# Activation tiles begin 64 bytes later in SBUF, weight tiles stay where they are

## The chip, the cores and the metric

One core of one Trainium2 chip runs the kernel. The metric is the device time of one execution in microseconds. Lower is better.

## The reference

Two transformer-like blocks on 512 tokens of width 1024, all in float32. In short:

```python
h = ln(ALPHA*x + 0.5*swiglu(x))                 # ffn1, 1024 -> 2816 -> 1024
h = ln(ALPHA*h + token_mixers(h))               # hgrn2 scan (4 heads) and spatial gating, then w_out
h = ln(ALPHA*h + cross_attention(h, ln(mem)))   # memory of 256 rows, 4 heads of 256
h = ln(ALPHA*h + 0.5*swiglu(h))                 # ffn2
z = modulate(h, c) @ w_in                       # second block: 11 slices of 512 and three gates of 1024
kc, vc = na_kv(modulate(ctx, c_ctx) @ w_in_kv)  # context of 256 rows
ya = neighbourhood_attention(q, k, v, kc, vc, rpb) * silu(..)
yb, yc = short_conv_branch(z), conformer_branch(z)
x = h + gate * ((ga*(ya@oa) + gb*(yb@ob) + gc*(yc@oc)) @ w_o)
```

Nearly all of the arithmetic is in the projections (`x @ w`).

## The kernel before

Activations are kept with features on the 128 partitions: a chunk is 128 features x 512 tokens, and `h` has 8 such chunks. The weights are streamed from HBM in strips of 128 x 1024 floats (512 KB), through a ring of four slots (`RING = 4`). There are some 300 strips. SyncE issues the load of a strip into `raw` when the strip four places before it has been split. ScalarE copies the strip to `w_hi` in the type fp32r (L407), and VectorE writes the remainder `raw - w_hi` to `w_lo` (L414). The activations are split in the same way into a `_hi` and a `_lo` tile.

A product of two float32 operands is then three fp32r matmuls, hi x hi, hi x lo and lo x hi, which accumulate in one bank of PSUM. All of them are issued by the helper `product`, in line L422. `feature_strip` runs the 8 blocks of a strip, so 24 matmuls: the 128 x 128 weight block is loaded into the array (the profile calls it PEld) and 512 or 256 columns of activations stream past it. In `token_strip` the roles are swapped, the activation block is loaded and the weights stream (`moving_weights`). In the names of the profile the moving operand stands first: `proj<-a_hi,w_hi` streams `a_hi` past `w_hi`.

The order of the work is written out by hand for each engine. TensorE goes through the strips in the order of the stream: gate and up of the first feed-forward (from 6 us), down, the mixer's projections with the scan's small matmuls between them, `w_out`, memory keys (`side_hi`, `side_lo`, 256 columns), memory values, queries, attention, `xa_w_o`, the context's keys (`ctx_hi`, `ctx_lo`, 256 columns, from 762 us), the second feed-forward, the context's values, twelve strips for each of four head pairs with the neighbourhood attention between them (up to 1462 us), the merge and `w_o`. The norms between the phases run on VectorE, ScalarE and GpSimd beside the last strips of the phase before; in some places a chunk is split into two halves of 256 tokens, which gives the 256-column matmuls of `a`, `hid` and `m`.

Tiles lie in SBUF in the order in which they are allocated. Tiles of an `ExitStack` named `ph` or `part` are released at its end, so the phases lie on top of each other, all behind `ctxv`. A tile takes its size in bytes for each partition, rounded up to 32. `raw`, `w_hi`, `w_lo` and `h` come first, 16,384 bytes each, and begin at an address that is a multiple of 128. `a_hi`, `a_lo` and then `cols` (271 floats, 1,084 bytes) follow. `consts` (1,024 bytes, its first half the identity) and the constant matrices behind it therefore begin at remainder 64 by 128. The small tiles behind them sum up so that `work`, `sq`, `ctxk`, `ctxv` and the tiles of all phases begin at remainder 0 again, with few exceptions: `ctx_hi` and `ctx_lo` at 64, behind `xs` with its 192 bytes, and in the attention phase the tiles from `glu` to `ns` at 32, behind `cv` with its 514 floats.

Of the kernel before, what the change touches and what calls it, by code (L numbers as in the profile page):

```python
# [20 lines left out]
F32 = mybir.dt.float32  # L21
# [6 lines left out]
P = 128  # L28
# [28 lines left out]
LEVELS = 7  # L57
RING = 4
SB = 8


S_FFN1 = 0
# [95 lines left out]
def hybrid_blocks(nc, stream, ada_in, cond_in, x_in, mem_in, ctx_in, cols_in, const_in, mask_in, rows_in, wst_in, band_in, rpb_in,  # L158
                  out):
    with ExitStack() as ctx:  # L160
# [3 lines left out]
        def sb(name, shape, dt=F32, scope=ctx):  # L164
            return scope.enter_context(nc.sbuf_tensor(name, shape, dt))
# [5 lines left out]

        raw = sb("raw", [P, RING, SB * P])
        w_hi = sb("w_hi", [P, RING, SB * P], F32R)
        w_lo = sb("w_lo", [P, RING, SB * P], F32R)
        h = sb("h", [P, KD, T])
        with ExitStack() as ph:
            cond_row = sb("cond_row", [P, 2, D], F32, ph)
            ada_prod = sb("ada_prod", [P, 2, D], F32, ph)
# [51 lines left out]
        with ExitStack() as ph:  # L230
            side = sb("side", [P, KD, M], F32, ph)
            side_hi = sb("side_hi", [P, KD, M], F32R, ph)
            side_lo = sb("side_lo", [P, KD, M], F32R, ph)
            xq = sb("xq", [P, KD, T], F32, ph)
            memk = sb("memk", [P, KD, M], F32, ph)
            memv_hi, memv_lo = (sb(n, [P, MB, W5], F32R, ph) for n in ("memv_hi", "memv_lo"))
            xp = sb("xp", [P, 2, 2, M], F32, ph)
            xpt_hi, xpt_lo = (sb(n, [P, 2, MB, M], F32R, ph) for n in ("xpt_hi", "xpt_lo"))
            xs = sb("xs", [P, 3, 8, 2], F32, ph)
            ctx_hi = sb("ctx_hi", [P, KD, M], F32R, ph)  # L240
            ctx_lo = sb("ctx_lo", [P, KD, M], F32R, ph)
        with ExitStack() as ph:
# [181 lines left out]

        def feature_strip(pe, st, g, xh, xl, first=0, blocks=SB, last=True, order=None, ready=None, n=T, blk0=0,
                          beside=None):

            pe.wait_ge(lo_ready, st.n + 1)
            if first == 0:
                ge(pe, proj_read[g.slot], g.turn)  # L430
            for j, k in enumerate(order or range(blocks)):
                if ready:
                    ready(k)
                if beside and k in beside:
                    beside[k]()
                at = (blk0 + k) * P
                mm = product(proj[:, g.slot, :n], w_hi[:, st.slot, at:at + P], w_lo[:, st.slot, at:at + P],
                             xh[:, first + k], xl[:, first + k], first == 0 and j == 0, last and j == blocks - 1)
            mm.then_inc(strip_done, 1)
# [483 lines left out]
        def pe_down(pe, s0, g0, hid0, m, beside):  # L923
            for c in range(KD):
                if c in beside:
                    beside[c]()
                for j in range(DOWN_STRIPS):
                    if c == 0:
                        pe.wait_ge(hid_l, hid0 + min(KF, SB * (j + 1)))
                    feature_strip(pe, Nth(s0 + c * DOWN_STRIPS + j), Nth(g0 + c), hid_hi, hid_lo, first=SB * j,  # L930
                                  blocks=min(SB, KF - SB * j), last=(j == DOWN_STRIPS - 1))
# [1814 lines left out]
```

## Time and profile before

| | |
|---|---|
| median of 3 runs | 1708.28 us (1707.93 to 1708.65) |
| profiled execution: span of its instructions | 1706.6 us |
| TensorE busy (matmuls) | 1691.5 us, 99% |
| weight loads, beside the matmuls | 1394.7 us, 82% |
| VectorE busy | 994.7 us, 58% |
| ScalarE busy | 683.6 us, 40% |
| GpSimd busy | 166.8 us, 10% |
| read from HBM | 182.9 MB, 110 GB/s |

The profile gives no other time for its own execution than the span. A matmul's end is modelled: successive matmuls of one strip overlap in the listing, each with a duration longer than its distance to the next one. So a full TensorE row says that matmuls followed each other without a pause, not that they went as fast as they can. For that one looks at the number of matmuls in a stretch, at the distance of their starts, or at differences of the durations.

### The profile page before, as it was taken

What the parts mean: (1) busy time and instruction counts of PE and PEld (TensorE: products, weight loads), DVE (VectorE), ACT (ScalarE), POOL (GpSimd) and SP (SyncE); (2) the same over time, 40 slices, a digit from 0 to 9 for tenths busy, and PEclk for the clock granted to TensorE, in tenths of its full rate; (3) what the DMA queues carried; (4) which work ended last, traced back from release to release, by engine and by line L of the source; (5) the groups of instructions that cost most, each with busy time, mean ns of one, the idle gap of its engine ahead of it and who ended that gap; (6) DMA issues with size and microseconds to landing.
All of it is one profiled execution on the core that took longest, in us unless ns stands there. A gap on an engine that the chain in (4) does not pass through costs nothing.

```text
span 1706.6 us, 22901 instructions
## 1 busy us (share of the span) xinstructions
PE 1691.5 (99%) x8500; PEld 1394.7 (82%) x8500; DVE 994.7 (58%) x1341; ACT 683.6 (40%) x975; POOL 166.8 (10%) x158
## 2 busy tenths in 40 slices
PE   9999999999999999999999999999999999999999
PEld 7888888888787888888888888877778787788887
DVE  5333339987965784666333333457976869844442
ACT  4222232246454465434222223346454445732330
POOL 0000000112004521013000000013011020000000
DMA  5333247633122353223332233323333222243331
GB/s 216 98 98 98 91 138 231 222 121 119 52 98 66 109 182 137 67 82 123 98 98 94 92 130 117 109 87 118 85 99 95 86 83 86 74 123 109 104 109 62
DMA packets 51476, 188.05 MB, mean 110 GB/s; under 512 B 5776, under 2 KB 6288, under 8 KB 50512
## 3 DMA queue, kind: packets, MB, share of 16 engines
q1 hardware_dynamic: 44640, 161.50, 29.7%
q10 hardware_dynamic: 5184, 16.00, 2.9%
q0 software_dynamic: 1584, 9.60, 1.6%
q8 instruction: 47, 0.77, 0.2%
q14 instruction: 21, 0.17, 0.0%
HBM read 182.89 MB, written 4.19 MB: 110 GB/s over the span
## 4 chain that ended last, share of the span: by engine, by line
PE 89%; DVE 7%; ACT 2%; issue 1%; DMA 0%; POOL 0%; SPq 0%; DVEq 0%; ACTq 0%; POOLq 0%
PE proj L422 83%; DVE w_lo L414 1%; PE aux L1859 1%; PE aux L1846 1%; PE aux L1619 1%; PE aux L1836 1%; DVE y L2016 0%; ACT w_hi L407 0%; DVE score L1221 0%; DVE qk L1264 0%; DVE md L1242 0%; PE aux L566 0%; DVE qk L1265 0%; PE aux L1839 0%; DVE md L1241 0%
## 5 line engine op out<-in xcount | busy, mean ns | idle before, releaser
L414 DVE TENSOR_TENSOR w_lo<-raw,w_hi 128x1024 fp32r<-128x1024 f32 x300 | 380.5, 1270 | 388.8 <-ACT w_hi L407 382.0
L422 PE MATMUL proj<-a_hi,w_hi 128*128 128x512 f32 (+1 forms) x1536 | 600.8, 391 | 3.3 <-DVE a_lo L909 1.8
L422 PE MATMUL proj<-a_hi,w_lo 128*128 128x512 f32 (+1 forms) x1536 | 591.3, 385 | 0.0
L422 PE MATMUL proj<-a_lo,w_hi 128*128 128x512 f32 (+1 forms) x1536 | 591.0, 385 | 0.0
L407 ACT ACTIVATE w_hi<-raw 128x1024 fp32r<-128x1024 f32 x300 | 315.3, 1053 | 233.4 <-PE proj L422 164.3
L422 PEld LDWEIGHTS proj<-a_hi,w_hi 128*128 128x128 f32 x1536 | 288.5, 188 | 67.9 <-issue 5.8
L422 PEld LDWEIGHTS proj<-a_lo,w_hi 128*128 128x128 f32 x1536 | 288.7, 188 | 58.4 <-issue 2.9
L422 PEld LDWEIGHTS proj<-a_hi,w_lo 128*128 128x128 f32 x1536 | 288.5, 188 | 58.5
L422 PE MATMUL proj<-hid_hi,w_hi 128*128 128x512 f32 (+1 forms) x374 | 142.6, 381 | 0.0
L422 PE MATMUL proj<-hid_hi,w_lo 128*128 128x512 f32 (+1 forms) x374 | 140.9, 377 | 0.0
L422 PE MATMUL proj<-hid_lo,w_hi 128*128 128x512 f32 (+1 forms) x374 | 140.8, 377 | 0.0
L971 ACT ACTIVATE hid_hi<-work 128x512 f32 (+1 forms) x44 | 27.8, 632 | 196.5 <-DVE work L988 196.5
L988 DVE TENSOR_TENSOR work<-sq,proj 128x512 f32<-128x512 f32 x44 | 30.2, 687 | 106.7 <-PE proj L422 106.7
L2016 DVE SCALAR_TENSOR_TENSOR y<-glu,wtap,y 128x512 f32 (+1 forms) x120 | 90.6, 755 | 3.2
L422 PEld LDWEIGHTS proj<-hid_hi,w_hi 128*128 128x128 f32 x374 | 70.4, 188 | 13.9 <-issue 0.7
L422 PEld LDWEIGHTS proj<-hid_lo,w_hi 128*128 128x128 f32 x374 | 70.4, 188 | 13.6 <-issue 0.7
L422 PEld LDWEIGHTS proj<-hid_hi,w_lo 128*128 128x128 f32 x374 | 70.4, 188 | 12.9
L966 ACT ACTIVATE sq<-proj 128x512 f32<-128x512 f32 x44 | 26.3, 597 | 114.9 <-PE proj L422 114.9
L993 DVE TENSOR_TENSOR hid_lo<-work,hid_hi 128x512 f32 (+1 forms) x44 | 30.5, 693 | 39.7 <-ACT hid_hi L971 39.7
L728 POOL TENSOR_SCALAR h<-h,cols 128x512 f32<-128x512 f32 x32 | 40.7, 1275 | 98.2 <-DVE a_lo L710 50.6
L1906 ACT ACTIVATE npr<-aux,ns 128x512 f32<-128x512 f32 x32 | 22.0, 689 | 48.0 <-DVE ns L2031 48.0
L580 POOL TENSOR_TENSOR work<-h 128x512 f32<-128x512 f32 x3 | 4.7, 1574 | 364.2 <-DVE h L646 364.2
(368 smaller groups left out, 2011.1 us busy)
## 6 DMA issues: line engine op xcount, KB each, us to landing
raw<-stream SPq DMA_DIRECT2D x303, 512.0 KB, 3.5
ctxk<-ada_in ACTq DMA_DIRECT2D x12, 512.0 KB, 3.7
ctxv<-ada_in ACTq DMA_DIRECT2D x12, 512.0 KB, 3.9
out<-h ACTq DMA_DIRECT2D x7, 256.0 KB, 2.0
h<-x_in SPq DMA_DIRECT2D x3, 512.0 KB, 8.7
btab<-rpb_in POOLq DMA_DIRECT2D x4, 384.0 KB, 3.5
cond_row<-cond_in ACTq DMA_DIRECT2D x1, 1024.0 KB, 5.9
side<-mem_in POOLq DMA_DIRECT2D x1, 1024.0 KB, 5.2
```

The costliest lines, as they stand in the source:

```text
L407: nc.scalar.activation(w_hi[:, st.slot], raw[:, st.slot], ACT.Copy).then_inc(hi_ready, 1)
L414: nc.vector.tensor_tensor(w_lo[:, st.slot], raw[:, st.slot], w_hi[:, st.slot].bitcast(F32), ALU.subtract).then_inc(lo_ready, 1)
L422: mm = nc.tensor.matmul(dst, a, b, start=start and n == 0, stop=stop and n == 2)
L728: nc.gpsimd.tensor_scalar(m.dst[:, c], m.dst[:, c], 1.0, m.shift(c), ALU.mult, ALU.add).then_inc(n_raw, 1)
L966: nc.scalar.activation(sq[:, j // 2], res, ACT.Silu).then_inc(proj_read[g.slot], 1)
L971: nc.scalar.activation(hc, work[:, j // 2], ACT.Copy).then_inc(hid_h, 1)
L988: nc.vector.tensor_tensor(work[:, j // 2], sq[:, j // 2], res, ALU.mult).then_inc(proj_read[g.slot], 1)
L993: nc.vector.tensor_tensor(a, work[:, j // 2], b.bitcast(F32), ALU.subtract).then_inc(hid_l, 1)
L1619: mm = nc.tensor.matmul(aux[:, u % 2, t * M:(t + 1) * M], xq[:, 2 * hd + kk, at:at + P], memk[:, 2 * hd + kk], start=(kk == 0), stop=(kk = ...
L1836: nc.tensor.matmul(aux[:, n, :M], nq[part, at], grid(nk[part], ROWS, BAND_AT[cb], BAND), start=True, stop=True)
L1906: nc.scalar.activation(npr[:, u % 2], aux[:, u % 2], ACT.Exp, bias=ns[:, 0, u:u + 1], accum_out=ns[:, 1, u:u + 1]).then_inc(u_exp, 1)
L2016: ins = nc.vector.scalar_tensor_tensor(dst, src, wtap[:, tap:tap + 1], dst, ALU.mult, ALU.add)
```

## The change

Two padding tiles are allocated and never used. The first one, 16 floats for each partition, stands behind `h` and moves everything allocated after it by 64 bytes. The second one stands in front of `ctx_hi` and `ctx_lo` alone. `raw`, `w_hi`, `w_lo` and `h` keep their places. No instruction is added, removed or moved.

```diff
+HALF_LINE = 16
...
         w_hi = sb("w_hi", [P, RING, SB * P], F32R)
         w_lo = sb("w_lo", [P, RING, SB * P], F32R)
         h = sb("h", [P, KD, T])
+        sb("half_line", [P, HALF_LINE])
         with ExitStack() as ph:
             cond_row = sb("cond_row", [P, 2, D], F32, ph)
             ada_prod = sb("ada_prod", [P, 2, D], F32, ph)
...
             xpt_hi, xpt_lo = (sb(n, [P, 2, MB, M], F32R, ph) for n in ("xpt_hi", "xpt_lo"))
             xs = sb("xs", [P, 3, 8, 2], F32, ph)
+            sb("half_line_ctx", [P, HALF_LINE], F32, ph)
             ctx_hi = sb("ctx_hi", [P, KD, M], F32R, ph)
             ctx_lo = sb("ctx_lo", [P, KD, M], F32R, ph)
```

## Rows read from the trace of the kernel before

**Rows 1.** Page, first part: busy us, share of the span, instructions
```profile
PE 1691.5 (99%) x8500; PEld 1394.7 (82%) x8500; DVE 994.7 (58%) x1341; ACT 683.6 (40%) x975; POOL 166.8 (10%) x158
```

**Rows 2.** The chain that ended last, shares of the span by line
```profile
by line: PE proj L422 82.9%; issue 1.3%; DVE w_lo L414 1.1%; PE aux L1859 1.0%; PE aux L1846 0.9%; PE aux L1619 0.6%; PE aux L1836 0.6%; DVE y L2016 0.5%; ACT w_hi L407 0.4%; DVE score L1221 0.4%; DVE qk L1264 0.4%; DVE md L1242 0.4%; PE au
```

**Rows 3.** Stretches: length, busy (x instructions), PEclk, DMA, GB/s; last two: L422
```profile
43.00:256.00 213.00, 213.00 (x942) 176.36 (x941) 73.61 (x78) 61.86 (x78) 0.00 (x0) 1.00 0.33 105
1172.00:1462.00 290.00, 289.95 (x1561) 230.50 (x1559) 231.15 (x349) 150.26 (x245) 38.11 (x41) 1.00 0.29 91
...
300.00:800.00 500.00, 435.98 (x2196) 363.49 (x2195) 1.00 0.35 114
1172.00:1462.00 290.00, 239.82 (x999) 184.65 (x997) 1.00 0.29 91
```

**Rows 4.** L422 by tile: ns min/median/max, starts, forms
```profile
L422 PE MATMUL proj<-side_hi,w_lo x64: 277/283/283, 589.0 to 617.2; 128*128 128x256 f32 x64
...
L422 PE MATMUL proj<-ctx_hi,w_lo x32: 276/276/281, 763.0 to 773.6; 128*128 128x256 f32 x32
...
L422 PE MATMUL proj<-a_lo,w_hi x1536: 280/389/402, 6.7 to 1651.3; 128*128 128x512 f32 x184, 128*128 128x256 f32 x8
...
L422 PE MATMUL proj<-hid_hi,w_hi x374: 278/389/792, 246.2 to 1136.2; 128*128 128x512 f32 x165, 128*128 128x256 f32 x22
...
L422 PE MATMUL proj<-m_hi,w_hi x72: 277/389/389, 1659.9 to 1703.4; 128*128 128x512 f32 x56, 128*128 128x256 f32 x16
```

**Rows 5.** Timeline: start us, us, what (side, then ctx)
```profile
600.83 0.28 PE L422 MATMUL proj<-side_hi,w_lo 128*128 128x256 f32 x1
...
603.83 0.28 PE L422 MATMUL proj<-side_hi,w_hi 128*128 128x256 f32 x1
...
764.75 0.28 PE L422 MATMUL proj<-ctx_hi,w_lo 128*128 128x256 f32 x1
...
767.59 0.28 PE L422 MATMUL proj<-ctx_hi,w_hi 128*128 128x256 f32 x1
```

**Rows 6.** Plain f32 matmuls: duration ns min/median/max, starts, forms
```profile
L1313 PE MATMUL aux<-score,mv x32: 270/275/275, 502.8 to 508.7; 128*128 128x128 f32 x32
...
L1619 PE MATMUL aux<-memk,xq x64: 377/379/382, 675.0 to 707.1; 128*128 128x256 f32 x64
...
L1846 PE MATMUL aux<-consts,npr x128: 270/272/331, 1200.8 to 1456.1; 128*128 128x128 f32 x128
...
L1874 PE MATMUL aux<-nsq,consts x8: 591/592/592, 1180.3 to 1408.1; 128*128 128x512 f32 x8
```

**Rows 7.** Groups of L422 by form: xcount, busy us, mean ns, idle before
```profile
L422 PE MATMUL proj<-a_hi,w_hi 128*128 128x512 f32 x1472 | 582.2, 396 | 1.0 <-DVE a_lo L710 0.7
...
L422 PE MATMUL proj<-y_hi,w_hi 128*128 128x512 f32 x96 | 37.4, 390 | 0.5 <-issue 0.5
...
L422 PE MATMUL proj<-w_hi,a_hi 128*128 128x512 f32 x80 | 33.3, 416 | 0.0
...
L422 PE MATMUL proj<-mix_h,w_hi 128*128 128x512 f32 x64 | 25.6, 399 | 0.2
...
L422 PE MATMUL proj<-a_hi,w_hi 128*128 128x256 f32 x64 | 18.6, 291 | 2.3 <-DVE a_lo L909 1.8 <-DVE w_lo L414 0.5
...
L422 PE MATMUL proj<-w_hi,side_hi 128*128 128x512 f32 x32 | 12.7, 395 | 0.0
```

**Rows 8.** Six stretches with waits: busy time of L422 alone
```profile
sum 199.00, PE 156.85 PEld 130.06; mean PE 26.14 PEld 21.68
```

**Rows 9.** Groups by line and form on VectorE and ScalarE
```profile
L414 DVE TENSOR_TENSOR w_lo<-raw,w_hi 128x1024 fp32r<-128x1024 f32 x300 | 380.5, 1270 | 388.8 <-ACT w_hi L407 382.0
...
L407 ACT ACTIVATE w_hi<-raw 128x1024 fp32r<-128x1024 f32 x300 | 315.3, 1053 | 233.4 <-PE proj L422 164.3
...
L2016 DVE SCALAR_TENSOR_TENSOR y<-glu,wtap,y 128x512 f32 x90 | 67.6, 751 | 2.4
...
L704 DVE SCALAR_TENSOR_TENSOR hm<-h,mod_a,work 128x512 f32<-128x512 f32 x8 | 5.9, 746 | 1.7 <-ACT work L348 1.7
```

## The prediction

> **What bounds the kernel now.** I read the page's first part first: TensorE is busy for 1691.5 of 1706.6 us, the next engine for 58% of the span [rows 1]. Then the chain that ended last: 82.9% of it, 1415 us, is one line, L422, the three matmuls of every weight block [rows 2]. Then stretches: in the first gate/up phase (43 to 256 us) line L422 alone fills all 213 us with 942 matmuls (226 to 227 ns each, as one cut by the window's edge counts or not; I use 226.7), at a granted clock of 1.00, which is the 2.4 GHz level [rows 3]. 512 columns at 2.4 GHz are 213.3 ns, so each matmul takes some 13 ns more than its columns. There is no wait to remove in such a stretch; only the spacing of the matmuls counts. Elsewhere VectorE comes near: 231 of 290 us in the second block's attention phase, where TensorE stays busy all the same [rows 3].
>
> **What the change does to the addresses.** The padding tile `half_line` is 16 floats, 64 bytes. It is allocated behind `raw`, `w_hi`, `w_lo` and `h`, whose sizes (16,384 bytes a partition each) keep them at remainder 0. `a_hi`, `a_lo`, `hid_*`, `side*`, `mix_*`, `m_*`, `y_*` have sizes that are multiples of 128, and what lies between them adds up so that today they begin at remainder 0 too. One pair does not: in front of `ctx_hi` and `ctx_lo` stands `xs`, 3 x 8 x 2 floats = 192 bytes, so this pair lies at remainder 64 already now. The second padding tile cancels the first one there: 64 + 192 + 64 gives 64 again. So the ctx projection is, in the trace of before, what nearly every other projection becomes: weights at 0, activations at 64. No instruction, wait, DMA or buffer is added or removed.
>
> **Price of one matmul.** The clean comparison is the memory K projection (`side`, remainder 0) against the context K projection (`ctx`, remainder 64): same weights ring, 256 columns, same order of three products. The durations are 283 against 276 ns at the median, and the extremes hardly overlap (277 to 283 against 276 to 281) [rows 4]. The ends are modelled, so I also take starts: 25 steps in 3.00 us (600.83 to 603.83), 120.0 ns each, against 25 steps in 2.84 us, 113.6 ns [rows 5]. The gain is 6.4 ns by starts, 7 ns by durations; I take 6.7. At 256 columns the excess over the columns (106.7 ns) is 13.3 ns, the same as at 512 columns; so it is a fixed cost of each matmul with its weight load, and the shift takes half of it. I therefore use 6.7 ns at 512 columns too, which no row shows: 226.7 becomes 220. Bounds for 512 columns: 0 (it helps the narrow ones only) and 13.3 (all of the excess). I stay with the middle since the excess is equal at both widths.
>
> A second kind of row points the same way. The plain f32 matmuls with 128 columns take 275 ns where both operands lie at remainder 0 (`score`, `mv`) and 272 where one is the table `consts`, at remainder 64 today behind the 1,084 bytes of `cols` (1,088 with rounding) [rows 6]. These pairs keep their relation, both are moved, so I price them at nothing; they only say that the remainders of the two operands against each other matter. One row speaks against a general rule: `memk` against `xq`, both at 0, 256 columns, takes 379 ns. From 128 to 512 columns the opposite pairs grow by 320 ns (272 to 592), so 107 for 128 more columns; 272 + 107 = 379. The wider matmul shows no penalty at equal remainders. It is my reason for the first rival.
>
> The Trainium skill (TensorE: Matmul & The Clock Gate, "Step-by-step: what each phase is for") says that TensorE reads SBUF through two independent ports, one for the moving operand and one for the weights. By that rule the two streams would not touch each other, no start address would matter, and the sum would be 0. The 283 against 276 ns of this trace [rows 4] speaks against it, so I give that result a small chance below.
>
> **How many matmuls.** L422 with 512 columns: 3 x (1472 + 330 + 96 + 80 + 64 + 56 + 32) = 6390, for `a`, `hid`, `y`, `w_hi` against `a_hi`, `mix`, `m` and `w_hi` against `side_hi`; each row stands for three products, and the forms of `hid` are counted on every second matmul (165 and 22 for 330 and 44). With 256 columns: 3 x (64 + 44 + 16) for `a`, `hid`, `m` and 3 x 64 of `side` = 564 [rows 4, 7]. Left out: 96 of `ctx` (already at 64) and 96 of attention times V (`xpt` against `memv` or `side`), where both operands move together. In 336 of the 6390 (`w_hi` against `a_hi` or `side_hi`) the weights ring is the moving side and the activation is loaded; the remainders differ there too after the change, and I count them the same (2.3 us if that is wrong). 6954 x 6.7 ns = 46.6 us.
>
> **What does not come through.** In six stretches TensorE waits for chains of VectorE and ScalarE: 350 to 372 (halved first norm), 420 to 476 (the scan levels), 565 to 608 and 685 to 712 (norms, memory softmax), 762 to 783 and 1172 to 1202. There a shorter matmul only makes TensorE arrive earlier at the same wait. 156.9 of these 199 us are under L422 [rows 8]. 6.7 of 226.7 ns is 3.0%, so 4.7 us of gain stand in them and I count all of it as lost (at best all is kept). In the attention phase behind them no idle time above the profile's threshold shows, but VectorE has 80% of the time, and each strip's split (L414) must come within four strips: I take off another 1 us. That leaves 41 us. The chain gives nearly the same by another way: 1415 us at 3.0% is 42 us, and somewhat more for the narrow matmuls.
>
> In the feed-forward phases nothing is late next: a strip of 24 matmuls goes from 5.44 to 5.28 us, while its two splits are 1.27 and 1.05 us on two engines [rows 9], and its load of 512 KB goes out ahead (mean traffic 105 GB/s) [rows 3]; 512 KB every 5.28 us is 99 GB/s.
>
> **VectorE, ScalarE, DMA.** Their operands move as well, often one at 0 (`h`) and one at 64. The nearest rows: the same operation on 128x512 takes 751 ns with an operand at remainder 32 (`glu`) and 746 with all at 0 [rows 9]. That bounds it at +0.7% of the 995 us of VectorE less the 380 of L414, whose tiles stay: +4.3 us if all were on the path, under 1 us at the few per cent it has there. The other end is an equal gain, since that row's difference may be noise. I take 0. The DMAs write rows of 1 KB and more at a start 64 bytes later; taken as 0.
>
> **Sum.** 46.6 - 4.7 - 1 = 41 us. The profiled execution's span is 1706.6 us; the median 1708.3 is 1.7 us above, which I keep. 1665.7 + 1.7 = 1667.4, say 1667.
>
> **Rivals.**
> 1. *Only the narrow matmuls gain*: the excess at 512 columns comes from something else. 564 x 6.7 = 3.8 us, 1704.5. For it: the 379 ns of `memk`. Against it: 13 ns at both widths. 6%.
> 2. *VectorE takes over* wherever it is dense: all of the gain in 300 to 800 and 1172 to 1462 is lost. L422 stands there for 436.0 + 239.8 = 676 us [rows 3], 3.0% is 20 us, so 46.6 - 20 = 26 us and 1682. For it: the chain's steps through VectorE. Against it: TensorE is busy 289.95 of 290 us in the second stretch. 12%.
> 3. *Nothing*: the ctx strips are quicker for another reason (what runs beside them), or by the port rule above. 1708. 6%.
> 4. *Slower*: the shifted stream meets the writers of the ring, which stay at 0, more than today's does. The disturbed L422 matmuls reach 398 to 402 ns against 389 [rows 4]; a split lasts 1.27 + 1.05 us of each 5.44 us strip, 43% [rows 9]. If each such matmul paid 9 ns and none gained, 6390 x 0.43 x 9 = +25 us, 1733. It decides when 0.43 x 9 = 3.9 ns exceeds the gain of one matmul. Against it: in the ctx strips, beside splits, the maximum is 281. 4%.
>
> That the shift does not arrive (tiles not where I think) is part of case 3. My case holds 72%, with its own range 1661 to 1675. The range: adding rival 2 takes it to about 1686, and the low end 1659 covers a slightly larger step at 512 columns with nothing lost. A difference under 0.2% (3.4 us) can't be told from none: faster 0.89, same 0.07, slower 0.04.
>
> **What would show it.** L422 with 512 columns: median 382 to 383 ns for 389 in every group, at 256 columns 276 for 283; `ctx` rows unchanged; 43 to 256 us holding some 970 matmuls, not 942; f32 rows at 272 and 275 as before; L414 and L407 unchanged. Wrong if the 512-column rows stay at 389, if `w_hi<-a_hi` ones differ from the rest, or if waits on L414 grow by more than the matmuls shrink.

## The result and the profile after

The changed kernel takes 1720.1 us (1719.3 to 1721.3) against 1708.5 us (1707.9 to 1710.7): ratio 1.0068, 95% interval 1.0053 to 1.0082. It is slower by 11.7 us where I forecast 41 us faster. The span of the profiled execution grew by 13.1 us, from 1706.56 to 1719.62.

The page's first part, as in [rows 1]:

```profile
PE 1705.8 (99%) x8500; PEld 1396.9 (81%) x8500; DVE 994.9 (58%) x1341; ACT 683.4 (40%) x975; POOL 166.8 (10%) x158
```

All of it is TensorE: busy 1705.8 for 1691.5 us, while VectorE, ScalarE and GpSimd stay within 0.3 us. The chain of waits is shifted further onto the product line, which is now L425: 84.3% of the span, 1450 us, for 82.9%, 1415 us [rows 2].

```profile
by line: PE proj L425 84.3%; DVE w_lo L417 1.0%; PE aux L1862 1.0%; issue 0.9%; PE aux L1849 0.9%; PE aux L1622 0.6%; PE aux L1839 0.6%; DVE score L1224 0.4%; DVE qk L1267 0.4%; DVE md L1245 0.4%; PE aux L1842 0.4%; PE aux L569 0.4%; DVE qk
```

The same stretches as in [rows 3] (length, then busy us and instructions of each engine, granted clock, DMA share, GB/s):

```profile
43.00:256.00 213.00, 213.00 (x932) 174.79 (x931) 73.73 (x77) 59.57 (x77) 0.00 (x0) 1.00 0.32 102
1172.00:1462.00 290.00, 290.00 (x1529) 230.01 (x1528) 230.90 (x346) 148.34 (x242) 39.64 (x44) 1.00 0.29 92
```

Both are as full as before, at a granted clock of 1.00. The first holds fewer matmuls, 932 for 942, so nothing new waits there; the matmuls follow each other more slowly. The 1529 for 1561 of the second can't be read in this way: its work begins 10 us later than before, so the same window shows other work. From matmul to matmul the work of this stretch takes only 1.2 us longer (starts in the two traces). Where the matmuls are slower, the durations say (min/median/max in ns), answering to [rows 4]:

```profile
L425 PE MATMUL proj<-a_lo,w_hi x1536: 278/392/628, 6.9 to 1664.2; 128*128 128x512 f32 x184, 128*128 128x256 f32 x8
...
L425 PE MATMUL proj<-y_hi,w_hi x96: 388/388/469, 1491.0 to 1672.2; 128*128 128x512 f32 x96
...
L425 PE MATMUL proj<-y_lo,w_hi x96: 392/392/392, 1491.2 to 1672.4; 128*128 128x512 f32 x96
...
L425 PE MATMUL proj<-y_hi,w_lo x96: 394/394/397, 1491.4 to 1672.7; 128*128 128x512 f32 x96
...
L425 PE MATMUL proj<-w_hi,a_hi x80: 393/398/800, 421.2 to 1167.5; 128*128 128x512 f32 x80
```

The medians were 389 in every group. In the shifted kernel the three products of one block differ: high activations with high weights 388, low activations 392, high activations with low weights 394. `y` shows it with hardly any scatter. Their mean is 391.3, so about 2.3 ns worse. Where the weights are the moving side (`w_hi,a_hi`) it is 398, so these differ from the rest: one of the signs of being wrong that I had named.

```profile
L425 PE MATMUL proj<-side_hi,w_lo x64: 276/279/416, 592.7 to 622.3; 128*128 128x256 f32 x64
...
L425 PE MATMUL proj<-ctx_hi,w_lo x32: 279/279/279, 769.5 to 780.4; 128*128 128x256 f32 x32
```

At 256 columns the shift does help, as forecast in sign: 279 for 283. But the context pair went from 276 to 279, though it kept its remainder by 128: it moved by exactly 128 bytes. This row speaks against my picture of a remainder by 128, but can't settle it alone, since the pair also changes its pace where its distance stays (`e1_pad192` below); `e2_pad128` settles it.

The plain f32 matmuls (`memk`, `score`, `consts`) stand where they stood in [rows 6], and so does the split of [rows 9] (out<-in, count, busy us, mean ns, idle before):

```profile
L1622 PE MATMUL aux<-memk,xq x64: 378/379/382, 680.8 to 713.1; 128*128 128x256 f32 x64
...
L1316 PE MATMUL aux<-score,mv x32: 272/275/275, 506.0 to 512.0; 128*128 128x128 f32 x32
...
L1849 PE MATMUL aux<-consts,npr x128: 270/272/331, 1210.8 to 1467.3; 128*128 128x128 f32 x128
```

```profile
L417 DVE TENSOR_TENSOR w_lo<-raw,w_hi 128x1024 fp32r<-128x1024 f32 x300 | 380.4, 1269 | 397.1 <-ACT w_hi L410 390.6
```

**The count.** From the starts in the two traces (a distance of 260 ns or more, of 150 ns or more at 256 columns, holds a pause: it stays out of the mean, and what it has above the mean counts as pause): the 6054 matmuls with 512 columns and resident weights went from 227.0 to 229.0 ns on the mean, +12.0 us. The 336 with moving weights went from 227.9 to 233.3, +1.8 us. The 564 narrow ones gained 2.5 ns, -1.4 us, the 96 of the context lost 4.2 ns, +0.4 us, all others together +0.1 us. The pauses sum up to 31.5 us before and 31.7 after. Together that is the 13.1 us by which the span grew.

### The profile page after: what moved, and what is told of

The parts are those of the page before. It is cut to its first block, busy times and chain, and to the rows that moved or that the text cites. A ratio compares the mean times of both kernels' runs of the same rounds, so it can differ in the third digit from the quotient of the medians.

```text
span 1719.6 us, 22901 instructions
## 1 busy us (share of the span) xinstructions
PE 1705.8 (99%) x8500; PEld 1396.9 (81%) x8500; DVE 994.9 (58%) x1341; ACT 683.4 (40%) x975; POOL 166.8 (10%) x158
## 3 DMA queue, kind: packets, MB, share of 16 engines
q1 hardware_dynamic: 44640, 161.50, 29.1%
HBM read 182.89 MB, written 4.19 MB: 109 GB/s over the span
## 4 chain that ended last, share of the span: by engine, by line
PE 91%; DVE 6%; ACT 2%; issue 1%; POOL 0%; DVEq 0%; ACTq 0%; POOLq 0%
PE proj L425 84%; DVE w_lo L417 1%; PE aux L1862 1%; PE aux L1849 1%; PE aux L1622 1%; PE aux L1839 1%; DVE score L1224 0%; DVE qk L1267 0%; DVE md L1245 0%; PE aux L1842 0%; PE aux L569 0%; DVE qk L1268 0%; ACT w_hi L410 0%; DVE md L1244 0%; ACT md L1272 0%
## 5 line engine op out<-in xcount | busy, mean ns | idle before, releaser
L425 PE MATMUL proj<-a_hi,w_hi 128*128 128x512 f32 (+1 forms) x1536 | 602.1, 392 | 2.8 <-DVE a_lo L912 1.8
L425 PE MATMUL proj<-a_hi,w_lo 128*128 128x512 f32 (+1 forms) x1536 | 595.4, 388 | 0.0
L425 PE MATMUL proj<-a_lo,w_hi 128*128 128x512 f32 (+1 forms) x1536 | 594.9, 387 | 0.0
L425 PEld LDWEIGHTS proj<-a_hi,w_hi 128*128 128x128 f32 x1536 | 288.7, 188 | 70.3 <-issue 5.8
L425 PEld LDWEIGHTS proj<-a_lo,w_hi 128*128 128x128 f32 x1536 | 288.7, 188 | 62.3 <-issue 2.9
L425 PEld LDWEIGHTS proj<-a_hi,w_lo 128*128 128x128 f32 x1536 | 288.7, 188 | 59.0
L425 PE MATMUL proj<-hid_hi,w_hi 128*128 128x512 f32 (+1 forms) x374 | 143.1, 383 | 0.0
L425 PE MATMUL proj<-hid_lo,w_hi 128*128 128x512 f32 (+1 forms) x374 | 141.4, 378 | 0.0
L425 PE MATMUL proj<-hid_hi,w_lo 128*128 128x512 f32 (+1 forms) x374 | 141.4, 378 | 0.0
L425 PEld LDWEIGHTS proj<-hid_lo,w_hi 128*128 128x128 f32 x374 | 70.2, 188 | 14.2 <-issue 0.7
L425 PEld LDWEIGHTS proj<-hid_hi,w_hi 128*128 128x128 f32 x374 | 70.2, 188 | 14.2 <-issue 0.7
L425 PEld LDWEIGHTS proj<-hid_hi,w_lo 128*128 128x128 f32 x374 | 70.2, 188 | 13.7
L2166 ACT ACTIVATE gate<-proj 128x512 f32<-128x512 f32 x24 | 14.3, 597 | 65.6 <-PE proj L425 65.6
```

Source lines behind the costliest of these rows:

```text
L425: mm = nc.tensor.matmul(dst, a, b, start=start and n == 0, stop=stop and n == 2)
```

## The experiments

Two questions were open: is it the distance between the two operands (theory A) or something else about the shift, and why does the narrow matmul not stand for the wide one. In what follows "distance d" is the start of the moving tile less the start of the loaded tile, by 256 bytes. Before, it is 0 for the operands of every such product, but 192 for the context pair (`ctx_hi` starts at 205,632 in each partition, `w_hi` at 32,896; the difference, 172,736, leaves 192 by 256). In the changed kernel it is 64, for the context pair too. Where the weights are the moving side, 64 turns into 192 (-64 by 256). In attention times V both tiles moved, so it stays 0.

### Three whole kernels with other paddings

`e1_pad192`:

```diff
         h = sb("h", [P, KD, T])
+        sb("pad", [P, 48])
...
+            sb("pad_ctx", [P, 16], F32, ph)
             ctx_hi = sb("ctx_hi", [P, KD, M], F32R, ph)
```

> Padding of 192 bytes behind h instead of 64, so activations begin 192 bytes past the weights' remainder by 256; the context pair, which in the kernel before lay 192 past the weights, gets 64 bytes of its own and stays there. Theory A (what counts is the distance between the two streams by 256 bytes or more, and 192 is the good one, as the 113.6 ns of the context rows of before): 512-column matmuls at 220 ns spacing instead of 226.7, 256-column ones at 113.6 instead of 120, 1665 to 1670 us. Theory B (the context rows of before were quicker for a reason of their place in the program, and any shift off remainder 0 costs, as the 1720 us of the 64 byte shift): 1715 to 1722 us, 512-column spacing 229 on the mean.

Measured: 1744.3 us, ratio 1.0207 (1.0193 to 1.0221). The stretch of the first gate/up phase, and rows by form (count, busy us, mean ns):

```profile
43.00:256.00 213.00, 213.00 (x915) 170.70 (x914) 72.77 (x76) 59.23 (x77) 0.00 (x0) 1.00 0.30 94
```

```profile
L424 PE MATMUL proj<-hid_hi,w_lo 128*128 128x512 f32 x330 | 130.3, 395 | 0.0
...
L424 PE MATMUL proj<-ctx_hi,w_lo 128*128 128x256 f32 x32 | 9.0, 281 | 0.0
```

915 matmuls for 942. Both expectations missed: distance 192, which is where the quick context rows of before lay, is worse than 64 for wide matmuls (hidden tiles 395 for 389). The context pair itself, still at distance 192, now takes 281 ns on the mean, 276 before. So a narrow matmul has no fixed time even at one distance.

`e2_pad128` has 32 floats in both places:

> Padding of 128 bytes behind h; everything has its remainder by 128 again but a distance of 128 by 256 to the weights. Theory A: a time of its own, different from 1708 us, spacing at 256 columns not 120 ns; 1690 to 1720 us. Theory B (remainder by 128 is what counts): 1708 us, all rows as before. The context pair is at distance 64, as in the changed kernel: 118 ns by A (as there), 113.6 by B.

Measured: 1739.4 us, ratio 1.0183 (1.0169 to 1.0197).

```profile
43.00:256.00 213.00, 213.00 (x919) 172.66 (x918) 73.37 (x77) 59.54 (x76) 0.00 (x0) 1.00 0.30 95
```

Theory B, as put here, is refuted: all activations have their old remainder by 128 and the kernel is 31 us slower. (The context pair lies at 192 here, not at 64 as I wrote in the expectation; it kept its 276 ns.)

`e3_all64` moves the weights and `h` too:

```diff
+        sb("pad", [P, 16])
         raw = sb("raw", [P, RING, SB * P])
...
+            sb("pad_ctx", [P, 16], F32, ph)
             ctx_hi = sb("ctx_hi", [P, KD, M], F32R, ph)
```

> Padding of 64 bytes in front of the ring too, so weights, h and activations all move by 64 bytes and keep their distance 0. Theory A (distance): 1708 us, 389 ns rows as before; the context pair is at distance 0 too and takes 120 ns spacing. Theory C (the absolute remainder of the activations counts): 1720 us, as the changed kernel.

Measured: 1708.4 us, ratio 1.0000 (0.9991 to 1.0009), 941 matmuls in the stretch, and the context pair, now at distance 0, at 283 ns like every narrow matmul at distance 0.

```profile
43.00:256.00 213.00, 213.00 (x941) 176.37 (x940) 73.77 (x78) 62.11 (x78) 0.00 (x0) 1.00 0.34 105
```

```profile
L424 PE MATMUL proj<-ctx_hi,w_lo 128*128 128x256 f32 x32 | 9.1, 283 | 0.0
```

A common shift of 64 bytes does not matter, and theory C falls. What counts in the change is the distance.

### The distances by themselves

`e4_sweep` leaves out the whole computation. Two weight tiles and 16 pairs of activation tiles at steps of 32 bytes; TensorE runs two strips of 24 matmuls for each, nothing runs beside. The letters a to p stand for distances 0, 32, ... 480.

```diff
+            for n in (T, M):
+                for c in LETTERS:
+                    xh, xl = mh[c], ml[c]
+                    for r in range(2):
+                        blocks = []
+                        for k in range(SB):
+                            at = slice(k * P, (k + 1) * P)
+                            col = slice(k % 2 * T, k % 2 * T + n)
+                            blocks += [(wh[:, at], xh[:, col]), (wh[:, at], xl[:, col]), (wl[:, at], xh[:, col])]
+                        mm = product(bank(), n, blocks)
```

> Only matmuls, nothing else of the kernel: the three products of a strip, the activation tiles at 16 distances of 32 bytes (0 to 480) to the weight tiles, with 512 and 256 columns and with the roles swapped; no other engine works beside. Theory A: spacing depends on the distance, with period 256 or 512: about 226.7 at 0, 229 mean at 64, 220 at 192 for 512 columns, 120, 118, 113.6 for 256. Theory D (the differences come from the engines and DMAs that write the ring beside the matmuls): flat, the same spacing at all 16 distances.

Rows by form for the high tile at distances 0, 64, 128, 160, 192 and 256 (`ha`, `hc`, `he`, `hf`, `hg`, `hi`; count, busy us, mean ns of one):

```profile
L178 PE MATMUL proj<-ha,wh 128*128 128x512 f32 x16 | 6.2, 389 | 0.0
...
L178 PE MATMUL proj<-hc,wh 128*128 128x512 f32 x16 | 6.2, 389 | 0.0
...
L178 PE MATMUL proj<-he,wh 128*128 128x512 f32 x16 | 6.3, 395 | 0.0
...
L178 PE MATMUL proj<-hf,wh 128*128 128x512 f32 x16 | 6.3, 396 | 0.0
...
L178 PE MATMUL proj<-hg,wh 128*128 128x512 f32 x16 | 6.3, 395 | 0.0
...
L178 PE MATMUL proj<-hi,wh 128*128 128x512 f32 x16 | 6.2, 389 | 0.0
```

0, 256 and the high tile at 64 are at 389, the others shown at 395 and 396. The duration of one tile hides the pattern over the three products, so here are the distances of the starts in that trace, as a mean over all three products (worked out from some 48 starts each):

| distance, bytes | 512 columns, ns | 256 columns, ns | 512, roles swapped, ns |
|---|---|---|---|
| 0 | 226.7 | 119.7 | 227.8 |
| 32 | 233.4 | 117.9 | 233.1 |
| 64 | 229.1 | 117.9 | 233.4 |
| 96 | 233.5 | 119.7 | 234.1 |
| 128 | 233.3 | 118.7 | 232.5 |
| 160 | 234.2 | 118.6 | 233.4 |
| 192 | 233.2 | 117.8 | 229.1 |
| 224 | 233.1 | 118.3 | 233.2 |

(In the last column the distance is still activations less weights; seen as moving less loaded it is the mirror image, and 192 becomes 64.) The eight distances from 256 on give the first two columns again within 0.2 ns and the third within 1 ns, so the period is 256 bytes. The 220 ns that theory A expected at distance 192 did not come, it is 233. Theory D falls: with no other engine at work, distance 64 costs 2.4 ns at 512 columns, and the order 226, 229, 232 of the three products is that of `y` above. At 512 columns every other distance than 0 is worse. At 256 columns 0 is the worst of them, or level with 96. That is the answer to the forecast: the sign turns between the two widths.

### Which tile, which width

`e5_sweep_parts` (matmuls only) tries widths, moves single tiles, and takes smaller steps. The letters a to d stand for distances 0, 64, 128 and 192. In the second loop only the low activations (`j`) are moved, in the third only the high ones (`k`), in the fourth only the low weights (`v`); the last one takes distances of 4, 8, 16 and 240 bytes.

```diff
+            for n in (512, 448, 384, 320, 256, 192, 128):
+                for c in LETTERS:
+                    strips(h[c], l[c], wl, n)
+            for c in LETTERS:
+                strips(i[c], j[c], wl, T)
+            for c in LETTERS:
+                strips(k_[c], m[c], wl, T)
+            for c in LETTERS:
+                strips(n_[c], o[c], v[c], T)
+            for n in (T, M):
+                for q in range(4):
+                    mm = strips(f[q], g[q], wl, n, FINE[q])
```

> Matmuls only, as in the first sweep, at distances 0, 64, 128 and 192. First with 512, 448, 384, 320, 256, 192 and 128 columns; then with 512 columns and only one of the three tiles moved: the low activations, the high activations, the low weights; last 512 and 256 columns at distances of 4, 8, 16 and 240 bytes. Theory A (a stream is slowed by the load of the next weights that runs beside it, and their distance counts): with only the low activations moved, the matmuls of the low activations change and those of the high ones stay at 227 ns; with only the low weights moved, the same ones change, since the low weights are loaded beside them. Theory E (what counts is how one moving tile follows the other): with only the low weights moved nothing changes. By width: distance 0 best at 512 (227 against 229 to 233), worst at 256 (120 against 118); where between them the order turns is open. 4 to 16 bytes: like 32 bytes, 233, if the exact distance counts; 227 if only the 32 byte line does.

Rows by form (mean ns last): `h` at distances 0 and 64 with 448 columns; `h` at 0 and 192 with 256; the low weights moved by 64 (`vb`) and the high weights beside them; a distance of 4 bytes (`fa`).

```profile
L189 PE MATMUL proj<-ha,wh 128*128 128x448 f32 x16 | 5.8, 365 | 0.0
...
L189 PE MATMUL proj<-hb,wh 128*128 128x448 f32 x16 | 5.8, 360 | 0.0
...
L189 PE MATMUL proj<-ha,wh 128*128 128x256 f32 x16 | 4.5, 283 | 0.0
...
L189 PE MATMUL proj<-hd,wh 128*128 128x256 f32 x16 | 4.4, 277 | 0.0
...
L189 PE MATMUL proj<-nb,vb 128*128 128x512 f32 x16 | 6.4, 398 | 0.0
...
L189 PE MATMUL proj<-nb,wh 128*128 128x512 f32 x16 | 6.2, 389 | 0.0
...
L189 PE MATMUL proj<-fa,wh 128*128 128x512 f32 x16 | 6.4, 400 | 0.0
```

Mean distances of the starts over the three products, in ns:

| columns | 0 | 64 | 128 | 192 |
|---|---|---|---|---|
| 512 | 226.7 | 229.2 | 232.4 | 233.3 |
| 448 | 202.5 | 200.2 | 204.0 | 202.1 |
| 384 | 173.4 | 173.2 | 175.8 | 174.7 |
| 320 | 146.4 | 146.7 | 146.6 | 146.6 |
| 256 | 119.7 | 117.9 | 118.7 | 114.0 |
| 192 | 111.2 | 111.7 | 111.7 | 111.7 |

No rule by width appears: distance 0 is ahead of 64 by 2.5 ns at 512 columns, behind it by 2.3 at 448, level with it at 384 and 320. With 192 columns or fewer all are at 111 to 112. 256 columns at distance 192 ran at 117.8 in the sweep before and at 114.0 here, so two paces are possible at one distance, as for the context pair.

Theories A and E both fail in their simple form. With only the low weights moved by 64, the three products take 228.2, 229.1 and 235.7 ns; with only the low activations moved 231.1, 232.2 and 232.6. In the same tile sets with nothing moved they settle, after six to nine uneven ones, at 226 and 227. One moved tile slows the matmuls that never touch it. At 512 columns a distance of 4 bytes gives 237 to 238 ns, worse than 32 or 64, 8 bytes 233.5, 240 bytes 235.9; 16 bytes gives 232. So the exact start counts, not the 32-byte line. At 256 columns the order is another one again: 4 bytes 123.2, the slowest of all, and 16 bytes 113.3, the quickest.

`e9_sweep_single` (matmuls only) takes the three products away.

```diff
+                for c in LETTERS:
+                    strips([(blocks(wh), chunks(h[c]))] * 3, n)
+                for c in LETTERS:
+                    strips([(fixed(wh), chunks(i[c]))] * 3, n)
+                for c in LETTERS:
+                    strips([(blocks(wh), chunks(j["a"])), (blocks(wh), chunks(k_[c]))] * 2, n)
+                for c in LETTERS:
+                    mm = strips([(blocks(wl), chunks(m[c])), (blocks(v[c]), chunks(m[c]))] * 2, n)
```

> Matmuls only, without the three products: (h) one moving tile at distance 0, 64, 128, 192 to the weights, whose blocks follow each other; (i) the same with one and the same weight block each time; (j) moving tiles that alternate between distance 0 and the given one, all weights from one tile; (m) weights that alternate between two tiles, the second one moved. Theory A (the stream against the load beside it): h and i alike and ranked as in the sweep (227, 229, 233, 233 at 512 columns); in j and m only the matmuls beside the moved pair change. Theory E (how one moving tile follows the other): h, i and m flat at 227, only j changes. Theory F (the chain as a whole settles at a pace, each pair's delay feeding the next): h ranked as in the sweep, in j and m both kinds of matmul change.

Four stretches of 10 us of part h, distances 0, 64, 128, 192 (busy us and instructions of TensorE and of the weight loads, then idle engines, clock, DMA):

```profile
42.50:52.50 10.00, 10.00 (x46) 8.29 (x45) 0.00 (x0) 0.00 (x0) 1.00 0.01 2
53.50:63.50 10.00, 10.00 (x45) 8.23 (x44) 0.00 (x0) 0.00 (x0) 1.00 0.00 0
64.50:74.50 10.00, 10.00 (x45) 8.11 (x44) 0.00 (x0) 0.00 (x0) 1.00 0.00 0
75.50:85.50 10.00, 10.00 (x45) 8.01 (x44) 0.00 (x0) 0.00 (x0) 1.00 0.01 2
```

The starts say 226.7, 229.2, 232.4 and 233.3 ns, and the same within 0.4 ns with one weight block throughout. So one moving tile and one weight tile are enough, and the activations' low and high parts have nothing to do with it. In part j, where tiles at distance 0 and 64 alternate, those at 0 take 233.2 and those at 64 228.9 ns; in part m with distance 0 and 64 the two kinds take 229.0 and 231.2. Both kinds change, as theory F said. And a tile can lose its own price: where tiles at 0 and 192 alternate, they take 228.5 and 225.1 ns, 226.8 on the mean, as quick as all at 0, though all at 192 take 233.3. The starts also show how: the distances repeat in cycles, 226, 227, 227 at distance 0 (a mean of 544 cycles of the 2.4 GHz level for 512 columns), and 226, 230, 226, 229, 232, 240, 230, 234 in part j. With only the low activations moved (`e5_sweep_parts`) a cycle has 15 matmuls. The chain of loads and streams settles into a repeating pace. What inside the memory or the array makes a pace slower was not measured.

### Does the table carry over to the whole kernel

`e6_hid192`:

```diff
         with ExitStack() as ph:
+            sb("pad_hid", [P, 48], F32, ph)
             hid_hi = sb("hid_hi", [P, KF, T], F32R, ph)
```

> The kernel before with only the hidden tiles of the two feed-forwards 192 bytes later. By the table of the sweep (distance 192: 233.3 ns at 512 columns for 227): 990 matmuls x 6.3 = +6.2 us, 132 narrow ones at 114 for 120 = -0.8 us, so 1713.8 us, and all other rows as before. If instead the writers of the ring or a wait were behind the loss, the time would not follow this count: 1708 to 1710 us or over 1716.

Measured: 1713.8 us (1713.4 to 1714.1), ratio 1.0030 (1.0019 to 1.0041). Rows by form:

```profile
L423 PE MATMUL proj<-a_hi,w_lo 128*128 128x512 f32 x1472 | 573.2, 389 | 0.0
...
L423 PE MATMUL proj<-hid_hi,w_lo 128*128 128x512 f32 x330 | 130.3, 395 | 0.0
...
L423 PE MATMUL proj<-hid_hi,w_lo 128*128 128x256 f32 x44 | 12.2, 276 | 0.0
```

`a` stays at 389, the wide `hid` matmuls take 395, the narrow ones 276 for 283. The kernel became 5.2 us slower (1708.5 for the kernel before in the same session) where the count gave 5.4. That the time itself fits to 0.1 us is partly luck: single runs of one kernel scatter by 1 us.

`e7_side192` moves the memory keys' pair; the second padding tile brings what follows back to its remainder by 256:

```diff
+            sb("pad_side", [P, 48], F32, ph)
             side_hi = sb("side_hi", [P, KD, M], F32R, ph)
             side_lo = sb("side_lo", [P, KD, M], F32R, ph)
+            sb("pad_xq", [P, 16], F32, ph)
             xq = sb("xq", [P, KD, T], F32, ph)
```

> The kernel before with only side_hi and side_lo 192 bytes later, the distance of the context pair. Memory keys: 192 matmuls with 256 columns at 113.6 instead of 120 ns, -1.2 us on TensorE; the 96 swapped ones with 512 columns at 229 instead of 227, +0.2 us. Theory A: 1707.4 us, too little to be told from 1708.4 by the time, but the rows show it. The norms beside this stage may take the rest: then 1708.4.

Measured: 1709.1 us (1707.4 to 1710.5), ratio 1.0002 (0.9993 to 1.0011): no difference can be told. The narrow rows did get quicker, from 119.8 to 115.4 ns between starts for the high activations with low weights (113.6 was expected), and the 96 with moving weights slower, 231 for 227 (229 was expected). That is worth about -0.8 us and +0.4 us, so nothing is left to collect here. Both misses have one form: the same tiles at the same distance ran at two paces within this one trace. The narrow strips began at 118 ns, dropped to 113.4 in the middle of a strip, and ran at 118 again after the next pause. The swapped ones with 512 columns ran at 233.3 ns between 618 and 629 us and in the cycle 226, 229, 232 between 674 and 688 us.

`e8_pad256` has 64 floats behind `h`:

> Padding of 256 bytes behind h, so all activations keep their remainder by 256 and move by 256 bytes. If the period is 256 bytes, as the two halves of the first sweep were alike: 1708.5 us, 389 ns rows, context pair 276. If 512 (or more) counts in the whole kernel: slower, up to the 1739 us of the 128 byte padding.

Measured: 1708.2 us, ratio 1.0001 (0.9992 to 1.0010).

```profile
43.00:256.00 213.00, 213.00 (x941) 176.46 (x940) 73.72 (x78) 61.82 (x78) 0.00 (x0) 1.00 0.32 105
```

941 matmuls in the stretch: the period of 256 bytes holds in the whole kernel.

No version beats the kernel before. For its wide matmuls it already has the best distance of those tried; only the alternation of 0 and 192 in the sweep was as quick.

## Why the prediction was wrong, step by step

- **What bounds the kernel**: right. TensorE's spacing alone decided; the count of the spacings gives the 13 us of the span, and the pauses sum up to the same.
- **The addresses**: half right. Everything moved as described, but I reduced them by 128. The period is 256, so "at 64 already" was true only by 128: the context pair lay at 192 by 256, not at 64. No row of the trace before showed the distance that the change makes.
- **Price of one matmul**: the step that failed. "I therefore use 6.7 ns at 512 columns too, which no row shows". The reason was that the excess over the columns is the same at both widths, 13.3 ns. At distance 0 that is so: it is 13.0 to 13.4 ns at 256, 320, 384 and 512 columns as well (15.8 at 448). But an equal excess at distance 0 does not mean an equal gain from a shift: at distance 64 the excess is 11.2 ns at 256 columns and 15.9 at 512, at 192 it is 7.3 or 11.1 and 20.0. Shown in its place: +2 ns at 512 columns with distance 64 (6054 of them) and +5.4 with the roles swapped (336), where I had 6.7 less for both. The price itself also belonged to another distance, 192. I called the extremes of the two durations hardly overlapping, and they do overlap (277 to 283, 276 to 281); the medians and the starts carry that difference.
- **The bounds** of that price, 0 and 13.3 ns, excluded a loss, with no reason given. A row that could have warned was there: `memk` at 256 columns without a penalty where the pairs with 128 columns had one. I read it as "wide ones gain nothing" and not as "the order may turn with the width".
- **The narrow matmuls**: right in sign, too large: 2.5 ns for 6.7.
- **The 336 with swapped roles**: I counted them the same, as the remainders "differ there too". They lost most, 5.4 ns, since the sign of the distance counts.
- **What does not come through**: I took off 5.7 us for waits. The sum of the pauses is as long as before (31.7 for 31.5 us), so the loss came through whole.
- **VectorE, ScalarE, DMA at 0**: right. The engines' busy times stay within 0.3 us, and the page has the same 182.89 MB read, at 29.1% of the span for 29.7% on the strips' queue.
- **Rivals**: 1 to 3 all assumed no matmul gets slower. The slower one (1733) alone had the sign, with the wrong mechanism (writers of the ring); the sweep without any writer shows the same spacing. No case was there for a distance that is worse than 0 by itself. The rule of the independent ports (Trainium skill, TensorE: Matmul & The Clock Gate, "Step-by-step: what each phase is for") gave 0, which is nearer than my forecast; but 227 against 233 ns with nothing but addresses changed shows that here the two streams do not go on without regard to each other. Whether they meet in the reads or behind them is open.

## What to carry to other kernels

A difference of spacing that is measured at one width, one distance and one order of operands holds for these alone. Before it is multiplied by thousands of matmuls of another width, measure that width; a kernel of matmuls only, with a table of tiles at all distances, costs one run, and from its table the loss of `e6_hid192` was counted as 5.4 us and measured as 5.2. When tiles that feed fp32r matmuls of 512 columns are laid out, keep the moving and the loaded tile at the same remainder by 256 bytes: a small table put in between costs 0.7 to 2.1% here.

## What the runs showed of the hardware

- The distance between starts of fp32r matmuls with 512 columns depends on the start address of the moving less the loaded operand, by 256 bytes: 226.7 ns at 0, 229.1 at 64, 232 to 234 at the other steps of 32 bytes, 237 to 238 at 4 bytes. Moving everything by 64 bytes makes no difference (1708.4 us).
- The effect changes sign with the width: 448 columns are quicker at 64 (200.2) than at 0 (202.5), 256 columns at 192 (114.0 or 117.8) than at 0 (119.7). With 192 and 128 columns a matmul takes 111 to 112 ns, whatever its columns and its distance.
- Two paces occur at one distance: near 113.5 and near 118 ns at 256 columns, and 229 and 233.3 ns at 512 columns (`e7_side192`, weights moving), with the same tiles. Which one a strip takes up was not found.
- The extra time is not a matter of the one matmul: moving one of three tiles changes the spacing of all, in cycles of 3 to 15 matmuls, and alternating distances 0 and 192 costs nothing (226.8 ns). What in the chip sets the cycle is open.
